# Softmax attention units: the order of two ScalarE steps, and the number of identity products at the entry

## The chip, the core and the metric

The kernel runs on one core of a Trainium2 chip. What is measured is the device time of one execution, in microseconds (us); lower is better. The time before is 1359.41 us, the median of 3 runs (1358.11 to 1360.12). The engines are called PE (TensorE, matrix products and transposes), ACT or ScalarE, DVE or VectorE, POOL (GpSimd) and SP (which issues DMAs). Each works through its own queue in order, and they wait for one another by semaphores.

## What is computed

One decoder layer for 1024 tokens of width 1024, in float32. The part that matters here is the softmax attention of four heads (the "MLA" group), with queries and keys of 192 (128 and 64 rotary) and values of 128:

```python
def causal_softmax_attention(q, k, v):
    S = q.shape[1]
    scale = MLA_QK_DIM ** -0.5
    outs = []
    for i in range(S // BLOCK_Q):          # blocks of 128 queries
        q0 = i * BLOCK_Q
        kend = q0 + BLOCK_Q
        s = jnp.einsum('bthd,bshd->bhts', q[:, q0:kend], k[:, :kend]).astype(jnp.float32) * scale
        causal = jnp.arange(kend)[None, :] <= (q0 + jnp.arange(BLOCK_Q))[:, None]
        p = jax.nn.softmax(jnp.where(causal, s, -jnp.inf), axis=-1)
        outs.append(jnp.einsum('bhts,bshd->bthd', p.astype(v.dtype), v[:, :kend]))
    return jnp.concatenate(outs, axis=1)
```

Ahead of it stand the input projection, the up-projection of queries and keys and their rotation; behind it a second kind of attention ("stick-breaking", eight heads), the output projection and a feed-forward part.

## The kernel before

The tokens lie in reverse order, so query block `qt` has 8 - `qt` key blocks of 128. Matrix products of full precision are made from three: each operand is split into a high part (a copy in the narrower format, made by ScalarE) and a low part (the difference, made by VectorE), and `three` sums high*high, high*low and low*high (lines L1691 to L1693).

**The softmax stage** is a loop over 32 units, written out by hand. A unit is one head and one query block: two phases `p` of 16 units `v` each, in the order of blocks 1, 7, 3, 5, 6, 4, 8, 2 for each head (`BLOCKS`). Unit `u` goes this way:

1. PE makes the scores (`mla_scores`) into a PSUM pair, banks 0 and 1 or 2 and 3 in turn. Scores `u` wait for exponential `u - 2`, which read that pair.
2. VectorE takes the negative row maximum `nmx` (L1393).
3. ScalarE takes the exponential into `pm` (L886), two buffers in turn, with the row sums in a second instruction. It waits for the maximum, and for the turn `u - 2`, which read that buffer.
4. PE turns (transposes) the blocks of `pm` into banks 4 and 5 (`mla_turn`, L1934). It waits for exponential `u` and for both copies of unit `u - 1`.
5. ScalarE copies bank 4 into `pmT` (`mla_copy`, L827), VectorE copies bank 5 (L1377; a unit of one block has none). `G0` is the number of blocks in ScalarE's half.
6. PE multiplies with the values (`mla_values`, L1945), and VectorE divides by the row sum (`mla_finish`).

PE's order is, for each `n`: scores `n + 2`, turn `n`, values `n - 1`. VectorE's is: maximum `u`, copy `u - 2`, finish `u - 3`, and a low split where there is one. ScalarE's is: exponential `u`, copy `u - 2`, and a high split where there is one (`SPLIT_AT`, and a few by name): the operands of the next head are split in between, 1024 columns at a time.

**The entry** to the stage: after the last of the eight up-projection tiles PE works off `WARM_MLA` products of a bf16 identity with itself into bank 0 (L1898), whose result nobody reads. Then it makes the scores of units 0 and 1, for which the first high and low splits must be there, turns the last tile of queries and keys (L1858 to L1862), and goes on with the scores of unit 2 once ScalarE and VectorE have brought that tile out (`turn_out`, L761, L774).

**Behind the stage** PE goes on to the stick-breaking units without a stop: their scores follow those of the last softmax units in the same loop, and ScalarE makes the last two softmax copies in its first two stick-breaking steps.

Of the kernel before, what the change touches and what calls it, by code (L numbers as in the profile page):

```python
# [106 lines left out]
NU = len(UNITS)  # L107
# [1 line left out]
QKL = {6: (0, 1), 7: (1, 1), 8: (0, 2), 9: (1, 2), 10: (2, 1), 11: (3, 1), 12: (2, 2), 13: (4, 1)}  # L109
NM, NS = MH // 2 * NU, SBH // 2 * NU  # L110
WARM = 40
WARM_MLA = 44
BLOCKS = [NT - i for _, i in UNITS]
G0 = [(b + 1) // 2 for b in BLOCKS]
G1_BEFORE = [sum(b > 1 for b in BLOCKS[:k]) for k in range(NU + 1)]
# [18 lines left out]
def build(nc, xT, cols_d, rows_d, pos_d, ada1_d, ada2_d, win_d, qup_d, kvup_d, wout_d, gu_d, down_d, x2_d, t_d, qkl_d, out_d):  # L134
# [155 lines left out]
    def pair(b, n=S):  # L290

        return ps[:, b:b + 2, :].rearrange("p b n -> p (b n)")[:, 0:n]
# [23 lines left out]
    def after(n):  # L316

        return n + 1 + PRIME
# [7 lines left out]
    def maxima(done, recips):  # L326

        return min(done, NM) + recips + PRIME
# [309 lines left out]
    def _(act):  # L638
# [103 lines left out]
        def mla_split(what, p, e, t=slice(0, S)):  # L742

            if p:
                act.wait_ge(sem["m_qk"], after(NU * (p - 1) + (7 if e == 0 else NU - 1)))
            dst, src = {"r": (mrH[p], QRK[:, p, t]), "q": (mqH[e], QN[:, 2 * p + e, t]), "k": (mkH[e], KN[:, 2 * p + e, t])}[what]
            A(dst[:, t], src, ACT.Copy).then_inc(sem["m_h"], 1)

        def rope_key_high(e):

            o = slice(64 * e, 64 * e + 64)
            A(KRH[e][o, :], QRK[o, 2, :], ACT.Copy).then_inc(sem["kr_h"], 1)

        def turn_out(tt):

            act.wait_ge(sem["tr_done"], after(tt))
            if tt == NT - 2:
                turn_rope(tt)
                act.wait_ge(sem["t_act"], 2 * tt + 1 + PRIME)
                mla_split("r", 0, 0, EARLY)  # L760
            A(QN[:, :, token_tile(tt)], ps[:, 4, :].rearrange("p (h n) -> p h n", h=MH), ACT.Copy).then_inc(sem["t_act"], 1)  # L761
            if tt < NT - 2:
                turn_rope(tt)
            elif tt == NT - 2:
                act.wait_ge(sem["t_act"], 2 * tt + 2 + PRIME)
                mla_split("q", 0, 0, EARLY)
                act.wait_ge(sem["t_dve"], after(tt))
                mla_split("k", 0, 0, EARLY)
            else:
                turn_rope(tt)  # L770
# [46 lines left out]
        def first_split(t):  # L817

            for what in "rqk":
                mla_split(what, 0, 0, t)  # L820

        def mla_copy(u, v):

            act.wait_ge(sem["m_tr"], after(u))
            act.wait_ge(sem["m_av"], after(u - 2))
            n = G0[v] * P
            A(pmT[v % 2][:, 0:n], ps[:, 4, 0:n], ACT.Copy).then_inc(sem["m_ta"], 1)  # L827
# [52 lines left out]
        def mla_step(u):  # L880

            p, v = divmod(u, NU)
            n = BLOCKS[v] * P
            act.wait_ge(sem["m_max"], maxima(u + 1, max(0, u - 3)))
            act.wait_ge(sem["m_tr"], after(u - 2))
            A(pm[v % 2][:, 0:n], pair(2 * (v % 2), n), ACT.Exp, bias=nmx[:, v:v + 1],  # L886
              accum_out=den[:, v:v + 1]).then_inc(sem["m_exp"], 1)
            if u >= 2:
                mla_copy(u - 2, (u - 2) % NU)
            if u == 0:  # L890
                turn_out(NT - 1)
            if u == 2:
                act.wait_ge(sem["t_act"], 2 * NT + PRIME)
                act.wait_ge(sem["t_dve"], after(NT - 1))
                first_split(LATE)
            if u == 4:
                rope_key_high(1)
            if (p, v) in SPLIT_AT:
                mla_split(*SPLIT_AT[p, v])
# [39 lines left out]
        for u in range(NM):  # L939
            mla_step(u)  # L940
# [743 lines left out]
    def _(pe):  # L1684
# [211 lines left out]
        pe.wait_ge(sem["q_copied"], NT)  # L1896
        for _ in range(WARM_MLA):
            mm(ps[:, 0, 0:P], identb[:], identb[:], start=True, stop=True)  # L1898
# [393 lines left out]
```

## Time and profile before

| what | value |
|---|---|
| median of 3 runs | 1359.41 us (1358.11 to 1360.12) |
| profiled execution, own time | 1355.37 us |
| its span (first to last instruction) | 1353.6 us |
| mean granted clock of PE | 0.998 of full |
| PE busy | 1299.7 us, 96% of the span |
| VectorE busy | 805.9 us, 60% |
| ScalarE busy | 557.8 us, 41% |
| softmax stage | about 311 to 430 us of the span |

All rows come from one profiled execution. A row of the timeline gives the start, the length, the engine, the line, the operation with its output and input, how many were merged, and in brackets how long the engine stood idle ahead of it and what released it. Instructions on one engine overlap a little, so one can start before the end of the one before. A granted clock of 1.00 is PE's full 2.4 GHz, 0.50 is 1.2 GHz. Times in the text are us from the start of the span.

### The profile page before, as it was taken

The page shows a single profiled execution, that of the slowest core. Times are in us where ns is not written, and L with a number is a line of the kernel's source. Part 1 is how long each engine was busy: PE and PEld are TensorE (multiplying, and loading weights), DVE is VectorE, ACT ScalarE, POOL GpSimd, SP SyncE. Part 2 cuts the span into 40 slices and gives each one's busy share as a digit, 9 for nine tenths or more (in the row PEclk, how much of TensorE's full clock was granted, in tenths as well). Part 3 has the DMA queues.
Part 4 walks back from the last instruction along what each step waited for, and adds up shares of the span by engine and source line. Part 5 has one row for each costly group of instructions (what it writes and reads, how often), then busy time and mean ns, then how long its engine had stood idle before and what let it go on. Part 6 is the DMA issues. An engine that isn't in the chain of part 4 may idle for free.

```text
span 1353.6 us, 17167 instructions
## 1 busy us (share of the span) xinstructions
PE 1299.7 (96%) x6708; PEld 1082.0 (80%) x6708; DVE 805.9 (60%) x1096; ACT 557.8 (41%) x912; POOL 63.7 (5%) x71
## 2 busy tenths in 40 slices
PE   3999999998999999999999999999999999999998
PEld 2688878896888888888767888888888888887886
DVE  7534667686557888953579666556665643334333
ACT  4512212685435788951364333333333322322221
POOL 1100200131000001000000000000000000001001
PEclk9999999999999999999999999999999999999999
DMA  9253445100011333501142221222212145447443
GB/s 380 102 207 136 181 173 183 47 1 1 2 40 40 78 79 79 188 16 47 45 173 93 94 94 54 87 94 94 70 71 94 62 163 178 149 140 264 140 147 125
DMA packets 38989, 149.25 MB, mean 110 GB/s; under 512 B 4352, under 2 KB 4480, under 8 KB 37376
## 3 DMA queue, kind: packets, MB, share of 16 engines
q1 hardware_dynamic: 36576, 139.80, 30.3%
q0 software_dynamic: 2336, 8.39, 1.7%
q8 instruction: 52, 0.85, 0.3%
q14 instruction: 25, 0.20, 0.1%
HBM read 117.77 MB, written 24.12 MB: 105 GB/s over the span
## 4 chain that ended last, share of the span: by engine, by line
PE 87%; DVE 6%; ACT 3%; issue 2%; DMA 1%; POOL 1%; SPq 0%; DVEq 0%; ACTq 0%; POOLq 0%
PE ps L2190 28%; PE ps L1702 13%; PE ps L1691 11%; PE ps L1693 10%; PE ps L1692 10%; PE ps L1967 3%; PE ps L1945 2%; PE ps L1954 2%; PE ps L1912 1%; DVE left L1414 1%; PE ps L1934 1%; PE ps L1913 1%; DVE beta L1419 1%; ACT omb L920 1%; DMA ada<-ada 1%
## 5 line engine op out<-in xcount | busy, mean ns | idle before, releaser
L1691 PE MATMUL ps<-TH,dWH 128*128 128x512 f32 x352 | 137.1, 390 | 0.9 <-DVE yst L1666 0.9
L1693 PE MATMUL ps<-TH,dWL 128*128 128x512 f32 x352 | 137.0, 389 | 0.0
L1692 PE MATMUL ps<-TL,dWH 128*128 128x512 f32 x352 | 137.0, 389 | 0.0
L2190 PE MATMUL ps<-h2H,slH 128*128 128x512 f32 x320 | 124.6, 389 | 0.0
L2190 PE MATMUL ps<-h2H,slL 128*128 128x512 f32 x320 | 124.5, 389 | 0.0
L2190 PE MATMUL ps<-h2L,slH 128*128 128x512 f32 x320 | 124.5, 389 | 0.0
L1625 DVE TENSOR_TENSOR TL<-traw,TH 128x512 fp32r<-128x512 f32 x44 | 30.5, 693 | 134.6 <-ACT TH L1048 134.6
L1028 ACT ACTIVATE slH<-ssum 128x512 fp32r<-128x512 f32 x80 | 50.4, 632 | 140.4 <-PE ps L2190 96.4
L1048 ACT ACTIVATE TH<-traw 128x512 fp32r<-128x512 f32 x44 | 27.8, 632 | 164.1 <-PE ps L1693 155.7
L1414 DVE TENSOR_TENSOR_SCAN left<-omb 128x255 f32<-128x255 f32 (+4 forms) x64 | 86.5, 1352 | 9.9 <-ACT omb L920 9.0
L1691 PEld LDWEIGHTS ps<-TH,dWH 128*128 128x128 f32 x352 | 66.1, 188 | 15.5 <-DVE yst L1666 1.3
L1693 PEld LDWEIGHTS ps<-TH,dWL 128*128 128x128 f32 x352 | 66.1, 188 | 13.8
L1692 PEld LDWEIGHTS ps<-TL,dWH 128*128 128x128 f32 x352 | 66.1, 188 | 13.4
L1967 PE MATMUL ps<-VS,wT 128*128 128x64 f32 x576 | 71.3, 269 | 0.1
L2190 PEld LDWEIGHTS ps<-h2H,slH 128*128 128x128 f32 x320 | 60.1, 188 | 12.7 <-issue 0.3
L2190 PEld LDWEIGHTS ps<-h2L,slH 128*128 128x128 f32 x320 | 60.1, 188 | 12.5
L2190 PEld LDWEIGHTS ps<-h2H,slL 128*128 128x128 f32 x320 | 60.1, 188 | 12.4
L1967 PEld LDWEIGHTS ps<-VS,wT 128*128 128x128 f32 x576 | 69.2, 192 | 0.2 <-issue 0.2
L1603 DVE TENSOR_TENSOR slL<-ssum,slH 128x512 fp32r<-128x512 f32 x80 | 54.9, 688 | 18.2 <-ACT slH L1028 18.2
L1125 DVE TENSOR_TENSOR WL<-raw,WH 128x1024 fp32r<-128x1024 f32 x34 | 43.2, 1269 | 32.4 <-ACT WH L648 32.3
L1603 DVE TENSOR_TENSOR slL<-sraw,slH 128x512 fp32r<-128x512 f32 x60 | 41.2, 689 | 35.4 <-ACT slH L1028 35.4
L1627 DVE TENSOR_TENSOR dWL<-draw,dWH 128x1024 fp32r<-128x1024 f32 x44 | 53.9, 1226 | 11.0 <-ACT dWH L1050 11.0
(325 smaller groups left out, 3030.4 us busy)
## 6 DMA issues: line engine op xcount, KB each, us to landing
ada<-ada SPq DMA_DIRECT2D x12, 2048.0 KB, 9.3
draw<-down SPq DMA_DIRECT2D x44, 512.0 KB, 3.7
sraw<-gu SPq DMA_DIRECT2D x20, 1024.0 KB, 5.9
raw<-win SPq DMA_DIRECT2D x22, 512.0 KB, 4.8
traw<-t_spill_d SPq DMA_DIRECT2D x44, 256.0 KB, 3.9
t_spill_d<-tst SPq DMA_DIRECT2D x20, 512.0 KB, 3.0
x_in<-xT SPq DMA_DIRECT2D x4, 1024.0 KB, 8.3
qkl_spill_d<-qkl SPq DMA_DIRECT2D x8, 512.0 KB, 3.4
```

What stands on the lines that cost most here:

```text
L1028: A(slH[q][:], operand(u, q), ACT.Copy).then_inc(sem["g_h"], 1)
L1125: V.tensor_tensor(WL[par % 2][:], raw[r % 2][:], WH[par % 2][:], ALU.subtract).then_inc(sem["split_l"], 1)
L1414: V.tensor_tensor_scan(left[v % 2][:, 1:n], omb[v % 2][:, 0:n - 1], omb[v % 2][:, 0:n - 1], 1.0, ALU.mult, ALU.bypass).then_inc(sem["s_sca ...
L1603: V.tensor_tensor(slL[q][:], operand(u, q), slH[q][:], ALU.subtract).then_inc(sem["g_l"], 1)
L1625: V.tensor_tensor(TL[d % 2][:], traw[d % 2][:], TH[d % 2][:], ALU.subtract).then_inc(sem["tl_done"], 1)
L1627: V.tensor_tensor(dWL[d % 2][:], draw[d % 2][:], dWH[d % 2][:], ALU.subtract).then_inc(sem["d_l"], 1)
L1691: mm(out, lh, rh, start=first, stop=False)
L1692: mm(out, lh, rl, start=False, stop=False)
L1693: return mm(out, ll, rh, start=False, stop=last)
L1702: last = mm(ps[:, b + hf, :], l[s][:, j * P:(j + 1) * P], cut(r, j, half(hf)), start=(j == 0 and k == 0), stop=(j == KD - 1 and k == 2))
L1967: last = mm(ps[:, bank, c:c + SBD], wT[v % 2][:, k * P:(k + 1) * P], VS[:, qt + k, (2 * i + e) * SBD:(2 * i + e + 1) * SBD], start=(k == 0 ...
L2190: last = mm(ps[:, Q_BANK[q], :], l[q][:, w], r[:, c, :], start=(c == 0 and k == 0 and q not in (Q_G2, Q_S4)), stop=(c == 3 and k == 2), sk ...
```

## The change

`WARM_MLA` becomes 84 instead of 44. In ScalarE's step of a softmax unit the copy of unit `u - 2` is put ahead of the exponential of unit `u` and of the waits of that exponential. The last two softmax copies, which are made in the first two stick-breaking steps, stay where they are.

```diff
@@ -109,7 +109,7 @@
 WARM = 40
-WARM_MLA = 44
+WARM_MLA = 84
@@ -881,12 +881,12 @@
 
             p, v = divmod(u, NU)
             n = BLOCKS[v] * P
+            if u >= 2:
+                mla_copy(u - 2, (u - 2) % NU)
             act.wait_ge(sem["m_max"], maxima(u + 1, max(0, u - 3)))
             act.wait_ge(sem["m_tr"], after(u - 2))
             A(pm[v % 2][:, 0:n], pair(2 * (v % 2), n), ACT.Exp, bias=nmx[:, v:v + 1],
               accum_out=den[:, v:v + 1]).then_inc(sem["m_exp"], 1)
-            if u >= 2:
-                mla_copy(u - 2, (u - 2) % NU)
             if u == 0:
                 turn_out(NT - 1)
```

## Rows read from the trace of the kernel before

**Rows 1.** The page: busy time of PE; shares by engine of the chain that ended last.
```profile
PE 1299.7 (96%) x6708; PEld 1082.0 (80%) x6708; DVE 805.9 (60%) x1096; ACT 557.8 (41%) x912; POOL 63.7 (5%) x71
...
PE 87%; DVE 6%; ACT 3%; issue 2%; DMA 1%; POOL 1%; SPq 0%; DVEq 0%; ACTq 0%; POOLq 0%
```

**Rows 2.** Stretches: length, busy time by engine, PE's clock, DMA share, GB/s.
```profile
312.80:316.20 3.40, 3.40 (x12) 2.69 (x11) 1.08 (x5) 0.46 (x2) 0.00 (x0) 0.50 0.00 0
...
320.00:430.00 110.00, 104.08 (x744) 91.22 (x743) 62.68 (x136) 48.29 (x112) 2.03 (x4) 1.00 0.11 25
```

**Rows 3.** Who waited for whom, 305 to 430 us: total us, times, longest.
```profile
ACT pm L886 <- DVE nmx L1393: 48.3, 21, 3.6
...
ACT pm L886 <- PE ps L1934: 12.3, 10, 2.1
...
PE ps L1934 <- ACT pmT L827: 3.2, 2, 2.2
...
PE ps L1934 <- ACT pm L886: 1.8, 5, 0.4
```

**Rows 4.** Timeline of PE at the entry.
```profile
305.54 2.62 PE L1898 MATMUL ps<-identb 128*128 128x128 bf16 x44
311.17 0.30 PE L1691 MATMUL ps<-mkH,mqH 128*128 128x128 f32 x1 [3.02 <-issue]
...
318.34 0.44 PE L1691 MATMUL ps<-mkH,mqH 128*128 128x384 f32 x1 [0.96 <-ACT QRK L774]
```

**Rows 5.** Timeline of VectorE and ScalarE at the entry.
```profile
309.99 1.08 DVE L1316 TENSOR_TENSOR mkL<-KN,mkH 128x896 fp32r<-128x896 f32 x1
...
317.42 0.60 ACT L761 ACTIVATE QN<-ps 128x512 f32<-128x512 f32 x1 [3.01 <-PE ps L1862]
```

**Rows 6.** Timeline of PE in the softmax stage: turns L1934, one scores start.
```profile
321.82 0.95 PE L1934 MATMUL ps<-ident,pm 128*128 128x128 f32 x7
...
326.86 0.47 PE L1691 MATMUL ps<-mkH,mqH 128*128 128x512 f32 x1
...
328.73 0.74 PE L1934 MATMUL ps<-ident,pm 128*128 128x128 f32 x5 [0.16 <-issue]
...
337.94 0.63 PE L1934 MATMUL ps<-ident,pm 128*128 128x128 f32 x4 [2.21 <-ACT pmT L827]
...
355.35 0.52 PE L1934 MATMUL ps<-ident,pm 128*128 128x128 f32 x3 [0.95 <-ACT pmT L827]
...
366.00 0.63 PE L1934 MATMUL ps<-ident,pm 128*128 128x128 f32 x4 [0.42 <-ACT pm L886]
```

**Rows 7.** Timeline of ScalarE in the softmax stage.
```profile
322.89 0.79 ACT L886 ACTIVATE pm<-ps,nmx 128x640 f32<-128x640 f32 x1 [1.10 <-DVE nmx L1393]
...
323.67 0.59 ACT L827 ACTIVATE pmT<-ps 128x512 f32<-128x512 f32 x1
324.15 1.06 ACT L747 ACTIVATE mqH<-QN 128x1024 fp32r<-128x1024 f32 x1
...
328.25 0.37 ACT L827 ACTIVATE pmT<-ps 128x256 f32<-128x256 f32 x1
328.65 1.05 ACT L752 ACTIVATE KRH<-QRK 64x1024 fp32r<-64x1024 f32 x1
...
337.36 0.48 ACT L827 ACTIVATE pmT<-ps 128x384 f32<-128x384 f32 x1
...
354.66 0.59 ACT L827 ACTIVATE pmT<-ps 128x512 f32<-128x512 f32 x1
```

**Rows 8.** Line L827: lengths in ns (least, median, most), first and last start.
```profile
L827 ACT ACTIVATE pmT<-ps x32: 267/426/592, 320.9 to 425.6; 128x128 f32<-128x128 f32 x8, 128x512 f32<-128x512 f32 x8, 128x256 f32<-128x256 f32 x8, 128x384 f32<-128x384 f32 x8
```

**Rows 9.** Timeline of VectorE in the softmax stage.
```profile
335.00 1.22 DVE L1393 TENSOR_REDUCE nmx<-ps 128x1 f32<-128x1024 f32 x1
336.13 0.55 DVE L1377 COPY pmT<-ps 128x384 f32<-128x384 f32 x1
...
353.76 0.55 DVE L1377 COPY pmT<-ps 128x384 f32<-128x384 f32 x1
```

## The prediction

> **What bounds the kernel now.** I read the page first: PE is busy 1299.7 of 1353.6 us and 87% of the chain that ended last lies on it [rows 1]. So a change is worth what it takes out of PE's idle time or gives back of PE's clock, and the question is where PE stands still near the two edits. The view by stretches puts both there: from 312.8 to 316.2 us PE is fully busy, at a granted clock of 0.50 (the 1.2 GHz level), and over the softmax stage, 320 to 430 us, at 1.00, with 104.08 busy of 110 us, so 5.9 us are idle [rows 2]. The view of who waited for whom names the idle time: PE's turn of the probabilities (L1934) waits 3.2 us in two places for the copy L827 and 1.8 us in five that are put down to the exponential L886. ScalarE itself waits 48.3 us for VectorE's maxima and 12.3 us, in ten places, for PE's turns [rows 3]. ScalarE has room, but in what order it works decides when PE goes on.
>
> All these stalls are of one kind. The turn of unit n needs the exponential n and both halves of the copy n-1 (ScalarE's L827, VectorE's L1377), since it overwrites the PSUM banks 4 and 5. In ScalarE's queue the copy n-1 stands behind the exponential n+1, which needs the maximum n+1. In the timeline the copy of 0.48 us that begins at 337.36 ends at 337.84 and PE starts at 337.94, after 2.21 idle; the copy of 0.59 from 354.66 ends at 355.25 and PE starts at 355.35, after 0.95 [rows 6, 7]. The five put down to the exponential start in the same way 0.10 us after the copy's end (one stands in [rows 6], 366.00, with 0.42 idle; they sum to the 1.8). The eighth, 0.16 us at 328.73, starts 0.11 after the end of the copy at 328.25 [rows 6, 7].
>
> **Edit 1, 40 more identity products.** 44 of them take 2.62 us from 305.54, so 0.06 us each; then PE stands still for 3.02 us until 311.17 [rows 4], because the split that the first scores need (DVE mkL) ends at 311.07 [rows 5]. 40 more at 2.46/44 = 0.056 each last 2.24 us and end near 310.4, 0.77 us ahead of that: they cost nothing, and that 0.77 is their cover (if the splits came 1 us earlier, they would cost 0.2). The idle stretch shrinks from 3.02 to 0.77. In this trace the clock falls once: 1.6 us after that 3.02 idle. After 2.21 idle (337.94) and 0.96 idle (318.34) it stays at 1.00 [rows 2, 4, 6], so I take it that it doesn't fall. What this gives: 3.40 us at half clock is 1.70 us of excess; I take 1.6, as the ends of the stretch are known only to about one matmul. It counts in full, since what comes next waits for this work: ScalarE's turn_out (317.42) waits 3.01 us for PE's transposes, the third unit's scores (318.34) wait for that [rows 4, 5]. From there everything is earlier together. Bounds: 0 (the clock falls anyway) to 1.7.
>
> The Trainium skill, "TensorE: Matmul & The Clock Gate", in the part on transposes, says that the transpose mode doesn't count as busy for the clock. By that rule the transposes and the pause ahead of 318.34 could bring on a fall of their own, now that the one before is gone. The trace speaks against it: the clock rose at 316.2 and stayed up across just those transposes and the pause of 0.96 us. By the rule the entry's gain would be near zero.
>
> **Edit 2, the copy ahead of the exponential.** Nothing is added: the same 32 copies and 32 exponentials run, no DMA and no other queue is passed, the splits stay behind both. The copy u-2 waits for the turn u-2, for which the exponential u waited too (its buffer), and for the values u-4, which PE has issued before that turn; so no new wait ends late. What changes:
>
> (a) The copy runs in the idle time ahead of the maximum, and no longer ends any of the eight waits. What is late next is VectorE's half of the copy, which stays behind the maximum, or PE's own work.
>
> (b) Where a split follows, it starts one copy earlier, and so do the low split and the next maximum, which close a ring (exponential, copy, split, low split, maximum, exponential).
>
> (c) Where the turn u-2 ends last, the exponential comes later by the copy: 0.27 to 0.59 us [rows 8].
>
> The long stall, step by step, in the times of before. The turn of unit 1 ends at 322.77 [rows 6]. Copy 1 now starts there instead of at 323.67, and the exponential of 322.89 moves 0.48 behind it (0.59 less the overlap of 0.11 seen between 323.67 and 324.15) to 323.30, 0.41 late. Three splits then lose the copy ahead of them: 0.48 (323.67 to 324.15), 0.40 (328.25 to 328.65), 0.37 (a copy of 384 columns, 0.48 as at 337.36, less 0.11) [rows 7]. The maximum of 335.00 comes at 335.00 + 0.41 - 1.25 = 334.16, VectorE's copy behind it at 336.13 - 0.84 = 335.29 and ends at 335.84 [rows 9]; with 0.10 PE could turn at 335.94. PE's own scores end at 335.73 (337.94 less 2.21), or 335.57 with the 0.16 of the first stall gone. So PE turns at 335.94 instead of 337.94: 2.0 us for the two stalls, with 0.4 left of the long one, ended by VectorE's copy.
>
> The 0.95 at 355.35: two splits lie ahead in its ring (0.16 + 0.16 for two copies of 0.27); VectorE's copy ends at 353.76 + 0.55 - 0.32 = 353.99 [rows 9]. PE's own end is 355.35 - 0.95 = 354.40, less 0.25 from the stall before it: 354.15. Both are there together: 0.95 gone, with nothing to spare. The five short ones, 1.8 in all: the turn that such a copy wants has ended well ahead of it, and VectorE is named in one wait of PE only, at the end of the stage; all gone. Sum: 2.0 + 0.95 + 1.8 = 4.7 us.
>
> Point (c) costs nothing by my reading: the exponential u is wanted by the scores u+2, and the closest case is the first: the exponential of 323.30 ends by 324.2 (0.79 long, and its sum), and its scores start at 326.86, 2.7 us later [rows 6]. Bounds: a gain of 5.1 (all stalls) to a loss, priced below. The handover to the next stage (one stall of 0.17 us by VectorE) and all behind it is chained to PE, and is carried along.
>
> In sum 1.6 + 4.7 = 6.3 us. Profiled, that is 1355.4 - 6.3 = 1349.1 us (span 1347.3). That execution lies 4.0 below the median of the runs shown; against the median the forecast is 1359.4 - 6.3 = **1353.1 us**, a change of -0.46%. A measurement of this kernel can tell about 0.2% (2.7 us) from no change.
>
> **The rivals.**
> - *The clock falls anyway*, by the page's rule or otherwise; only edit 2 works: 1359.4 - 4.7 = 1354.7. For it: one fall in the trace is thin evidence, and the timed runs may stand differently. Against: 0.77 us idle is less than pauses without a fall. 12%.
> - *The waits move to VectorE.* The ring doesn't shorten, only ScalarE's copy does: the long stall ends at 336.68 + 0.10 with VectorE's copy (gain 1.2 of 2.2), the next at 354.41 (0.9), the short ones go (1.8), the first stays: 3.9, with the clock 5.5: 1353.9. If half of the short ones stay also: 3.0, with the clock 4.6: 1354.8. For it: VectorE's copy and splits stand behind maxima, next in line everywhere. 14%.
> - *The gain is given back in the next stage*, where ScalarE and VectorE are busy for most of the time: what is early there waits for them. Then only some 1.5 us are left: 1357.9, no change by the bound. Against: those engines' work there starts from PE's scores too, nothing is tied to an absolute time. 8%.
> - *Slower: the exponential takes the copy's place.* The ten exponentials that wait for PE's turn come a copy later, ten times 0.43 (the median copy [rows 8]) = 4.3 us, if the scores or the turn n have no slack for it; then the stalls at the turn aren't recovered either. 1359.4 + 4.3 - 1.6 = 1362.1; without the clock 1363.7; all 32 copies on the path would make 13.6 and 1371. It decides once the slack of 2.7 us at the closest place is less than a copy. Against: it is over four times the longest copy. 6%.
>
> **How the numbers follow.** My forecast: 60%, its own range 1352.0 to 1354.4 (clock 1.2 to 1.7, stalls 4.0 to 5.1, 0.5 of scatter). The range reaches over the first two rivals and the scatter of the runs: 1351.0 to 1356.6, leaving out the last two and a little of the rest. Faster by over 0.2% (below 1356.7) holds in the forecast and two rivals, 0.85 less a little for mixed cases; within 0.2% 0.1; slower 0.06.
>
> **What would show it.** Right: 84 products end near 310.4 with under 1 us idle behind; the clock is 1.00 from 308 to 320; the third unit's scores start near 316.7; PE's waits for L827 in the softmax stage are gone, and what is left there (0.4 us) is put down to VectorE's L1377; the copy begins before the exponential; ScalarE's idle time stands ahead of both. The stage's idle time is some 1.2 us instead of 5.9. Wrong: a clock below 1 after 312 us; waits of PE on L886 with a true length; more idle time after 430 us.

## The result, and the profile after

The changed kernel takes 1349.11 us, the median of 4 executions (1348.95 to 1351.58); the kernel before took 1359.74 beside it (4 executions, 1358.11 to 1360.12). The ratio is 0.9934, with a 95% interval of 0.9915 to 0.9953. It isn't the quotient of the two medians, which is 0.9922: by the medians the gain is 10.6 us, by the ratio 9.0 (6.4 to 11.6). The forecast was 1353.1 with a range of 1351.0 to 1356.6: the direction was right, the gain was above the 6.3 forecast either way, and the time lies outside the range. The profiled execution, though, has a span of 1347.4 us, and the prediction had said 1347.3 for it. So profile against profile the forecast holds, and median against median it doesn't. That gap is what the experiments are about.

The page's row of busy time: PE's 1298.9 us are nearly those of [rows 1], in a shorter span.

```profile
PE 1298.9 (96%) x6748; PEld 1082.6 (80%) x6748; DVE 805.8 (60%) x1096; ACT 559.9 (42%) x912; POOL 63.7 (5%) x71
```

Stretches of the changed kernel, against [rows 2] (length; busy time of PE, PEld, DVE, ACT, POOL; PE's clock; DMA share; GB/s):

```profile
312.80:316.20 3.40, 3.40 (x23) 2.88 (x21) 2.46 (x7) 0.46 (x2) 0.00 (x0) 1.00 0.00 0
320.00:430.00 110.00, 107.37 (x783) 94.91 (x782) 68.49 (x143) 54.61 (x117) 2.03 (x4) 1.00 0.11 25
```

The clock stays at 1.00 over the entry, and PE is busy 107.37 us of the second stretch instead of 104.08 (it now reaches some 8 us into the next stage). Who waited for whom, 305 to 430 us, and in the last row over the whole span for PE (total us, times, longest):

```profile
ACT pmT L827 <- PE ps L1934: 37.4, 25, 3.1
...
ACT pm L888 <- DVE nmx L1393: 14.9, 16, 1.7
...
PE ps L1934 <- DVE pmT L1377: 1.0, 2, 0.8
```

PE no longer waits for ScalarE's copy or exponential (L886 is now L888); both rows on PE in [rows 3] are gone. ScalarE's idle time now stands ahead of the copy, which waits for its turn, where it costs nothing. The view names two waits of PE in the stage, both for VectorE's half of the copy. Over the stretch from 320 to 430 us PE is idle for 2.63 us; 1.47 of these stand in three pauses of the next stage (0.62 at 421.38, 0.49 at 425.30 and 0.36 at 428.05), which leaves 1.16 where 1.2 was forecast. PE's timeline, against [rows 4] and [rows 6]:

```profile
306.07 4.85 PE L1898 MATMUL ps<-identb 128*128 128x128 bf16 x84
311.70 0.30 PE L1691 MATMUL ps<-mkH,mqH 128*128 128x128 f32 x1 [0.78 <-issue]
...
317.33 0.44 PE L1691 MATMUL ps<-mkH,mqH 128*128 128x384 f32 x1 [0.96 <-ACT QRK L774]
...
335.10 0.63 PE L1934 MATMUL ps<-ident,pm 128*128 128x128 f32 x4 [0.85 <-DVE pmT L1377]
...
347.76 0.95 PE L1934 MATMUL ps<-ident,pm 128*128 128x128 f32 x7
...
351.28 0.52 PE L1934 MATMUL ps<-ident,pm 128*128 128x128 f32 x3
...
361.35 0.60 PE L1934 MATMUL ps<-ident,pm 128*128 128x128 f32 x4
...
421.38 0.30 PE L1954 MATMUL ps<-ident,beta 128*128 128x128 f32 x1 [0.62 <-issue]
```

This gives the gain of each part by the start times of the same instruction in both traces. The first scores come 0.53 us later than in the kernel before (311.70 against 311.17); the identity products already start that much later (306.07 against 305.54), so it comes from the stages ahead, where nothing was changed. From them to the third unit's scores it is 5.63 us instead of 7.17: 1.54 from the clock. From there to the first stick-breaking turn, which stood at 428.00 before, it is 104.05 instead of 109.66: **5.61 from the new order**. Behind that 0.4 is lost again, in a wait of PE for a weight split. A wait of this kind, 0.4 to 0.6 us long, stands in six of the thirteen traces, two of the old order (e1, g3) and four of the new, and is missing in the other seven: it is scatter. 0.53 - 1.54 - 5.61 + 0.4 = -6.2, the difference of the spans. That this meets the forecast of 6.3 is partly luck: the new order brought 0.9 more than its share of the sum, and 0.9 of scatter took it away again.

```profile
428.00 0.30 PE L1954 MATMUL ps<-ident,beta 128*128 128x128 f32 x1 [0.51 <-issue]
```

### The profile page after: what moved, and what is told of

It is laid out like the page before. It is cut to its first block, busy times and chain, and to the rows that moved or that the text cites. A ratio compares the mean times of both kernels' runs of the same rounds, so it can differ in the third digit from the quotient of the medians.

```text
span 1347.4 us, 17247 instructions
## 1 busy us (share of the span) xinstructions
PE 1298.9 (96%) x6748; PEld 1082.6 (80%) x6748; DVE 805.8 (60%) x1096; ACT 559.9 (42%) x912; POOL 63.7 (5%) x71
## 4 chain that ended last, share of the span: by engine, by line
PE 85%; DVE 7%; ACT 3%; issue 2%; DMA 2%; POOL 1%; SPq 0%; DVEq 0%; ACTq 0%; POOLq 0%
PE ps L2190 28%; PE ps L1702 13%; PE ps L1691 10%; PE ps L1693 10%; PE ps L1692 10%; PE ps L1967 3%; PE ps L1954 2%; PE ps L1945 2%; PE ps L1912 1%; DVE left L1414 1%; PE ps L1913 1%; PE ps L1934 1%; DMA traw<-t_spill_d 1%; DVE beta L1419 1%; ACT omb L920 1%
```

## The experiments

The kernel before ran 59 times beside the experiments, on three chips. Its times, grouped by the mean clock of the execution, already say where the missing 4 us are:

| mean clock of PE | executions of before | time, us |
|---|---|---|
| 0.998 | 15 | 1355.2 to 1356.0 |
| 0.996 | 16 | 1356.9 to 1358.7 |
| 0.995 | 12 | 1357.8 to 1358.8 |
| 0.994 | 16 | 1359.3 to 1360.8 |

The profiled execution of the kernel before was one of the first row. An estimate from the table: 0.998 less 0.994, of 1357 us, is 5.4 us of clock, and the executions of the last row are 4.6 us longer (medians 1360.1 and 1355.5). The mean clock is a rough guide, though, as it also counts a fall that costs nothing: in every trace the clock goes to 0.50 once more behind PE's last product, 2.0 to 5.3 us after its end, when PE has nothing left to do. In the trace of the changed kernel that product ends at 1341.15:

```profile
1344.00:1346.00 2.00, 0.00 (x0) 0.00 (x0) 0.00 (x0) 0.00 (x0) 0.00 (x0) 0.50 0.38 145
```

In the kernel before it starts at 1350.45, so its trace has two falls and not one, and its 0.998 is both of them together. The theories:

- **A**: in the timed executions the clock falls in more places than the profile showed; which of them, varies. The change takes places away.
- **B**: the gap of 4 us between profile and median is a matter of chip or execution and has nothing to do with the change.

### One part alone

**e1**, only the first edit, in the kernel before:

```diff
-WARM_MLA = 44
+WARM_MLA = 84
```

> Only the 84 identity products; the copy stays behind the exponential. Theory A (the timed executions of before lose time to clock falls that its profiled one doesn't show, and the shorter idle time at the entry takes some of them away): clearly more than 1.6 us, some 4 to 6 us below before, and a mean clock of the timed executions of before that is lower than the 0.998 of its profile. Theory B (the 4 us between profile and timed executions of before are a matter of the chip or of the execution and have nothing to do with the change): 1.5 us below before. In the profile of both theories: third unit's scores 1.5 us sooner after the first scores, the eight stalls in the softmax stage as before.

Measured: 1357.64 us, 12 executions of 1356.10 to 1359.13, clock 0.996 to 0.998; before 1358.55 (1355.25 to 1360.80). Ratio 0.9994 (0.9984 to 1.0005). Neither the 4 to 6 us of A nor the 1.5 of B: 0.9 us by the medians, nothing that can be told from no change. Its trace shows that the entry isn't the only place. PE's timeline and two stretches of e1:

```profile
336.81 0.63 PE L1934 MATMUL ps<-ident,pm 128*128 128x128 f32 x4 [2.21 <-ACT pmT L827]
...
312.80:316.20 3.40, 3.40 (x22) 2.75 (x21) 2.47 (x6) 0.46 (x2) 0.00 (x0) 1.00 0.00 0
...
336.20:340.60 4.40, 3.79 (x21) 3.83 (x22) 1.08 (x4) 1.34 (x6) 0.00 (x0) 0.63 0.00 0
```

The fall at the entry is gone (1.00), and there is one behind the long stall of 2.21 us: a mean of 0.63 over 4.4 us is 3.3 us at half clock. So A needs a wider form: there are more places than the entry, and closing this one gives far less than 4 us. Whether the fall at the long stall stood there instead of the one at the entry, or would have been there in any case, one trace can't show; e4 below has both. The prediction had taken just this pause, because the clock held after it in the one trace, as a sign that such a pause is harmless.

**e2**, only the second edit, with 44 products (the diff of the change without its first hunk).

> Only the copy ahead of the exponential, with 44 identity products. By the change's own profile this part brings 5.6 us (the shift of PE between the third unit's scores and the first long stick-breaking turn). Theory A: 5.6 us, or more if a clock fall in the timed executions of before belongs to the 2.2 us stall at 338. Theory B: 5.6 us, and e1 and e2 add up to what before loses in its profile, not to the 10.6 us measured. The clock falls once after the entry, as in before.

Measured: 1352.67 us, 6 executions of 1348.52 to 1355.14, clock 0.993 to 0.999. Ratio 0.9948 (0.9931 to 0.9964), which is 7.1 us of 1358.55; by the medians it is 5.9. Both fit A (5.6 or more), and 5.9 fits B's 5.6 as well. B's sum doesn't decide either: e1 and e2 add up to 6.8 us by the medians and 7.9 by the ratios, against the 6.2 between the two profiled executions and the 10.6 measured. The fastest of the six took 1348.52 with a clock of 0.999. The profiled execution was the slowest. PE's timeline and two stretches:

```profile
32.48 0.77 PE L1770 MATMUL ps<-hH,WH 128*128 128x512 f32 x1 [2.16 <-ACT hH L666]
...
315.22 0.44 PE L1691 MATMUL ps<-mkH,mqH 128*128 128x128 f32 x1 [3.02 <-issue]
...
32.00:38.70 6.70, 5.62 (x20) 1.76 (x20) 3.02 (x4) 3.73 (x4) 0.00 (x0) 0.51 0.97 405
...
315.40:321.00 5.60, 5.60 (x19) 4.69 (x20) 2.49 (x9) 1.36 (x3) 0.00 (x0) 0.50 0.01 3
...
320.00:322.00 2.00, 2.00 (x9) 1.90 (x8) 0.27 (x1) 0.00 (x0) 0.00 (x0) 0.53 0.00 0
```

Two things are new. There is a third place, near 30 us, which neither kernel's first profile showed: a pause of 2 us in the input stage, and 6.8 us at half clock that begin inside it, at 31.8. And a fall at the entry can be 6.8 us long (315.1 to 321.9), not 3.4, though the pause ahead is the same 3.02 us: from the first scores to the third unit's it is 8.69 us in this trace, 7.17 in the kernel before and 5.63 without a fall.

**e4**, the kernel before with no products at the entry (`WARM_MLA = 0`).

> The kernel before with no identity products at the entry at all: PE stands still for 5.5 us instead of 3.0. Leaves no part of the computation out. The clock falls at least as long: Theory A: also in the timed executions a longer or earlier fall, 1 to 4 us slower than before. Theory B: 0 to 2 us slower, one fall.

Measured: 1359.86 us, 12 executions of 1356.69 to 1360.42, ratio 1.0005 (0.9994 to 1.0016). By the medians it is 1.3 us slower, which fits both theories. Its trace has falls in all three places (from 32.0, 311.9 and 342.6 us, the last behind the long stall, which ends at 341.48 here). The 44 products of the kernel before, which leave 3 us idle behind them, were worth nothing that can be told from no change.

### The places filled one by one

PE's idle time can be filled with identity products that nobody reads, without a change to what the other engines do. So each place can be closed alone.

**f1**, the changed kernel once more, on another chip.

> The changed kernel once more, beside the kernel before on one chip. By the profiles so far the clock can fall in three places: at 30 to 38 us (near the kernel's start, in the traces of e2, e3 and e4), at the stage's entry near 312 and behind the long stall near 338. Theory A: the changed kernel can only fall in the first: some executions at 1349.0 with a mean clock of 0.999, others 2 to 4 us above with 0.996 to 0.998, median 1349 to 1351; ratio to before 0.993 to 0.995. Theory B (execution scatter is something else than the clock): time and mean clock of the executions don't go together.

Measured: 1350.99 us (1350.13 to 1351.95, 5 executions, clock 0.997 to 0.999) beside 1358.07 of before (15 executions, 1355.30 to 1360.28). Ratio 0.9945 (0.9932 to 0.9959): 7.1 us by the medians, within 1 us of the forecast's 6.3. Median and ratio are where A had them, and time and clock go together, but none of the five was as fast as 1349.0. Its trace has one fall, near 30 us (this stretch):

```profile
32.00:38.00 6.00, 5.18 (x28) 1.95 (x27) 3.37 (x4) 2.36 (x3) 0.00 (x0) 0.72 0.98 407
```

So the 1349.11 of the first comparison was partly luck. Three of its four executions took 1348.95 to 1349.15 with a clock of 0.999; the one of them that was profiled has no fall in the input stage, and by their times the other two had none either. And none of the four of before was of the fastest kind (1358.11 was the lowest).

**f2**, the kernel before with 84 products, and the long stall filled:

```diff
+            if n == 5:
+                for _ in range(38):
+                    mm(ps[:, 3, 0:P], identb[:], identb[:], start=True, stop=True)
             turned(n)
```

> The kernel before with 84 products, and 38 more identity products into the free bank 3 ahead of the turn of unit 5, where PE stands still 2.2 us (2.1 us of products, hidden in that wait). The order on ScalarE is the old one and all eight stalls keep their length. Theory A: the clock no longer falls near 338; executions without a fall near the start take 1353.8 (1355.4 less 1.6), the others 1356 to 1358, median 1.5 us or more below e1 (1357.6). Rival: the clock doesn't fall there because of the pause, or the products delay the turn: 1357 to 1358 as e1.

Measured: 1355.98 us, 11 executions of 1354.20 to 1357.23. Ratio 0.9985 (0.9976 to 0.9994), against e1's 0.9994. As A expected, 1.7 us below e1's median, though on another chip (1.2 us by the ratios, whose intervals overlap), and the lowest time is at 1354. Its trace has a fall near 30 us and none at 338.

**f3**, the changed kernel with the pause near 29 us filled:

```diff
+        for _ in range(30):
+            mm(ps[:, 0, 0:P], identb[:], identb[:], start=True, stop=True)
         pe.wait_ge(sem["split_l"], 2)
         for n in range(KD + LAG):
```

> The changed kernel with 30 identity products (1.7 us) in PE's pause of 1.9 us near 29 us, the only place left where its clock fell before the end. Theory A: all executions at 1349.0 to 1349.5 with a clock of 0.999, median up to 1.5 us below the changed kernel's on this chip. Rival: the fall there stems from the stretch of products with one column ahead of the pause, or the 30 products end late: as the changed kernel or up to 0.5 us slower.

Measured: 1348.77 us, 5 executions of 1348.26 to 1349.15, all with a clock of 0.999. Ratio 0.9928 (0.9914 to 0.9941). 2.2 us below f1 on the same chip, and the two don't overlap (f1's lowest is 1350.13). That is more than the 1.5 expected, and the rival, that the products of one column ahead bring on the fall whatever stands in the pause, is refuted: f3's trace has no fall near 30.

**g1**, the old order with all three places filled (the additions of f2 and f3 together).

> The kernel before (old order on ScalarE) with all three pauses filled by identity products: 30 near 29 us, 84 at the stage's entry, 38 ahead of the turn of unit 5. Theory A: no fall in any execution, all within 1 us of 1354.2, mean clock 1.000 or 0.999; the difference to f3 (1348.8), 5.4 us, is then the pure worth of the new order, and the 5.5 us of scatter of the kernel before are gone. If a good part of the scatter stays, it isn't the clock's.

Measured: 1354.33 us, 11 executions of 1353.84 to 1355.05, ratio 0.9980 (0.9971 to 0.9989). The kernel before ran from 1355.24 to 1359.97 on the same chip: a spread of 4.7 us has become 1.2. This is the plainest evidence for A: nothing but PE's idle time was filled. In g1's trace the clock is 1.00 from PE's first product to its last, which ends at 1346.30. It falls only behind that, at 1348.28, and this alone makes the mean 0.998, below the 1.000 or 0.999 expected; the two slowest executions, 1354.67 and 1355.05, have 1.000. The products stand in the old stall and delay nothing: the turn behind them comes 19.61 us after the third unit's scores, against 19.60 in the kernel before. The products:

```profile
334.62 2.29 PE L2077 MATMUL ps<-identb 128*128 128x128 bf16 x38
```

It also gives the two parts apart. Without falls the old order takes 1354.33 and the new one 1348.77 (f3): 5.6 us, as the two first traces have it (5.61). The two ran on different chips; by their ratios, 0.9980 and 0.9928, it would be 0.5% or 7 us, with intervals of 1.2 and 1.8 us to either side.

**g2**, the new order, 44 products at the entry, the pause near 29 us filled.

> The new order with 44 products at the entry, and 30 near 29 us: only the entry is left as a place of falls. Theory A: a fall there in every execution, of 3.4 us (1.6 lost) or twice as long as in the trace of e2 (3.3 lost): 1350.4 to 1352.2, so 1.6 to 3.4 us above f3; this is what 84 instead of 44 are worth in the new order.

Measured: 1350.43 us, 5 executions of 1350.18 to 1351.91, clock 0.997 to 0.999, ratio 0.9956 (0.9940 to 0.9972); 1.7 us above f3, which ran on another chip. By its median the range was just met (1350.4 to 1352.2, and the lowest is below it), but not the "every execution": PE's timeline and a stretch of its profiled execution show the pause of 3.02 us with no fall behind it.

```profile
312.45 0.30 PE L1691 MATMUL ps<-mkH,mqH 128*128 128x128 f32 x1 [3.02 <-issue]
...
312.00:320.00 8.00, 6.59 (x41) 5.64 (x42) 5.46 (x13) 4.11 (x9) 1.83 (x2) 1.00 0.00 1
```

That execution took 1350.18 us all the same, 1.3 us more in span than f3's profiled one (1348.4 against 1347.1). 0.3 of it is there by the first scores and 0.6 is a wait of PE for a weight split in the last stage, which f3's trace doesn't have. So there is scatter of about 1 us that isn't put down to the clock, and the 1.7 us of g2 can't all be put down to the entry's falls.

**g3**, the kernel before with only the pause near 29 us filled.

> The kernel before with 30 products near 29 us: entry and the long stall are left as places of falls. Theory A: 1355.3 to 1358.5, median 1.5 to 2 us below before; the highest times of before, 1359.8 to 1360.8 with a clock of 0.994, are gone, since they need a fall near the start as well.

Measured: 1356.34 us, 11 executions of 1355.73 to 1359.39, ratio 0.9993 (0.9983 to 1.0003), beside 1357.48 of before. Ten of the eleven lie below 1357, but one at 1359.39 stands above what was expected, and the gain of 1.1 us is less than the 1.5 to 2 expected; the ratio can't be told from 1. That one has the same clock, 0.997, as executions of 1355.73 and 1355.83: its 3 us aren't the mean clock's, and what they are isn't shown. Its trace has no fall at the entry and one behind the long stall. Filling one place of three moves the median by about 1 us, as in e1. The three add up: 0.9 us for the entry (e1), 1.1 for the input stage (g3), 1.2 for the long stall (f2's 2.1 less e1's 0.9), in sum 3.2, all by the medians on their own chips; all three at once gave 3.15 (g1, 1357.48 to 1354.33). Each by itself is at the edge of what can be told from no change.

### The wait that is left

**e3** and **f4**: the changed kernel, and f3, with VectorE's copy of unit 4 ahead of the maximum of unit 6:

```diff
+            if u == 6:
+                mla_copy((u - 2) // NU, (u - 2) % NU)
             dve.wait_ge(sem["m_qk"], after(u))
             V.reduce_max(nmx[:, v:v + 1], pair(2 * (v % 2), n), axis=AX.X, negate=True).then_inc(sem["m_max"], 1)
-            if u >= 2:
+            if u >= 2 and u != 6:
                 mla_copy((u - 2) // NU, (u - 2) % NU)
```

> The changed kernel, and VectorE's copy of unit 4 ahead of the maximum of unit 6, the one place where PE still waits (0.85 us) for VectorE's copy. If that copy is all that stands in the way, PE turns at its own end: 0.8 to 1.0 us below the changed kernel, some 1348.2. Rival: the maximum of unit 6, 0.5 us later, makes the exponential and what hangs on it late, and nothing or less is left of it.

> f3 and the edit of e3 (VectorE's copy of unit 4 ahead of the maximum of unit 6). If the 0.85 us of PE's wait are worth their length: 0.8 us below f3, near 1348.3, and the best of all. Rival: the later maximum gives it back: as f3.

Measured: e3 1350.62 us (1348.00 to 1352.76, 6 executions), ratio 0.9940 (0.9924 to 0.9957), with a fall near 30 us in its trace; beside f1's 1350.99 on another chip nothing is decided. f4 1348.46 us (1347.93 to 1348.99, 5 executions), f3 1348.77 on the same chip; both have the ratio 0.9928. In f4's trace the turn of unit 5 no longer waits, and two rows on a new wait stands there:

```profile
333.98 0.61 PE L1938 MATMUL ps<-ident,pm 128*128 128x128 f32 x4
...
336.13 0.33 PE L1693 MATMUL ps<-mkH,mqH 128*128 128x128 f32 x1 [0.21 <-ACT pm L888]
```

From the third unit's scores to the turn of unit 6 it is 19.71 us in f4 (317.22 to 336.93) and 20.26 in f3: 0.55 of the 0.85 remain as a gain, and the scores of unit 8 now wait for the exponential of unit 6, which the later maximum delays. That is the rival's mechanism, at part of its price. f4 had the lowest median of all kernels, 9.6 us below the kernel before on its chip, but its 0.3 us over f3, where 0.8 was expected, are within the scatter.

## Why the prediction was right or wrong

**Which waits the new order removes: right.** All eight stalls were put down to the copy behind the exponential, and all are gone. ScalarE's timeline of the changed kernel has the order, against [rows 7], VectorE's the ring:

```profile
321.80 0.60 ACT L827 ACTIVATE pmT<-ps 128x512 f32<-128x512 f32 x1 [1.18 <-PE ps L1934]
322.30 0.79 ACT L888 ACTIVATE pm<-ps,nmx 128x640 f32<-128x640 f32 x1
...
323.07 1.06 ACT L747 ACTIVATE mqH<-QN 128x1024 fp32r<-128x1024 f32 x1
...
332.39 0.49 ACT L827 ACTIVATE pmT<-ps 128x384 f32<-128x384 f32 x1 [0.29 <-PE ps L1934]
334.52 1.11 ACT L888 ACTIVATE pm<-ps,nmx 128x1024 f32<-128x1024 f32 x1 [1.64 <-DVE nmx L1393]
```
```profile
333.27 1.22 DVE L1393 TENSOR_REDUCE nmx<-ps 128x1 f32<-128x1024 f32 x1
334.40 0.55 DVE L1377 COPY pmT<-ps 128x384 f32<-128x384 f32 x1
```

The exponential of unit 3 starts 0.50 behind its copy, where 0.48 was reckoned. The time frame has moved by 1.01 us (318.34 to 317.33). The ring's steps gave 334.16 for the maximum and 335.94 for the turn; less 1.01 these are 333.15 and 334.93, and the trace has 333.27 and 335.10. That VectorE's copy is next in line was right too (0.85 us left instead of 0.4: PE's own work ended 0.3 sooner, and the turn came 0.17 later). The rival in which the ring doesn't shorten is refuted by the same rows, and so is the slower rival: PE waits nowhere for the exponential in the changed kernel.

**The sum of the stalls: 4.7 forecast, 5.6 measured.** The first two gave 1.83 (2.0 forecast), the one of 0.95 gave 0.82, as PE's turn of that unit is at 351.28 instead of 355.35 and the one before it at 347.76 instead of 351.01. The five short ones are the term that was mis-sized. They were priced at their idle time, 1.8 in all. By start times they gave 0.42, 0.59, 0.41, 0.59 and 0.58, 2.6 in all, each 0.16 more than its idle time. The reason is in the rows: a product of 128 columns lasts 0.27 us in the view, but the next starts 0.11 later when none waits, so the last of a group still counts as busy for 0.16 us of a wait. Besides, the view prints no idle time below some 0.15 us (0.16 is the least in these rows), so a wait of some 0.3 us by start times can be missing from it. One such was in the kernel before, ahead of the turn of unit 19: 0.14 us are idle there, without a bracket, and its distance from the turn ahead fell from 3.66 to 3.34 (before, then after):

```profile
382.31 0.49 PE L1934 MATMUL ps<-ident,pm 128*128 128x128 f32 x3
...
385.97 0.74 PE L1934 MATMUL ps<-ident,pm 128*128 128x128 f32 x5
```
```profile
377.22 0.49 PE L1934 MATMUL ps<-ident,pm 128*128 128x128 f32 x3
...
380.56 0.71 PE L1934 MATMUL ps<-ident,pm 128*128 128x128 f32 x5
```

1.83 + 0.82 + 2.59 + 0.32 = 5.56; the rest, to 5.61, is rounding and small shifts. The stall of 0.95 doesn't fit the rule of 0.16: its removal should have given 1.11. The missing 0.29 is such a hidden wait that is left in the changed kernel. From the turn at 347.76 to that at 351.28 it is 3.52 us, where the same pair takes 3.24 in the last head (399.90 to 403.14), and PE starts 0.14 behind the end of VectorE's copy (350.59 + 0.55), as it does at 335.10, 0.15 behind the end of the copy that starts at 334.40. The prediction had PE and that copy ready together, "with nothing to spare"; the copy is late by this much.

**The clock at the entry: right in the trace, wrong as a rule.** The prediction reads that the clock falls once; it falls twice, but the second time behind PE's last product, where it costs nothing. 1.6 us were forecast for the first, 1.54 in the trace. The 84 products end 0.78 us ahead of the scores (0.77 forecast). That the clock doesn't fall behind transposes and the pause of 0.96 us held as well: it is 1.00 there in the changed kernel, with no fall ahead of it. So the rule of the Trainium skill that transposes don't count ("TensorE: Matmul & The Clock Gate", the part on transposes) had no effect here that could be seen, over ten transposes and one pause. But the step "falls after 3.02 us idle, holds after 2.21" failed both ways. In the traces of e1 and g3 the clock fell after the 2.21, in those of g2 and g3 it held after the 3.02.

**From the profile to the median: the step that failed.** The prediction carried the 4.0 us between the profiled execution and the median of before over to the changed kernel as a constant. They were falls of the clock in places that this one execution had been spared. The slower executions of before were not traced themselves; that it was falls rests on the table, on the traces of e1, e2 and e4, and on g1, where filled pauses took them away. The change closes two of the three places: none of the five traces with both edits (the changed kernel, e3, f1, f3, f4) has a fall at the entry or near 335. With g1 and f3 as the times without falls, the typical loss is 1357.8 - 1354.3 = 3.5 us before (median of 59 executions) and 1350.3 - 1348.8 = 1.5 us after (median of the 9 executions of this kernel). So the change is worth 5.6 us by its order and 2.0 by the clock, in sum about the 7.5 between the two medians, as far as times from different chips can be set beside each other; the forecast of 6.3 was 1.2 short, 0.9 of it in the stalls and the rest in the clock. The other 3.1 of the 10.6 measured at first are the draw of four executions each.

**The gain given back in the next stage:** refuted. From the first stick-breaking turn to the end it is 926.0 us after and 925.6 before, and the 0.4 is the wait for the weight split.

## What to carry to other kernels

When the profiled execution isn't near the median, ask for the difference before forecasting across it: compare the mean clock of all executions, not one trace. Price a stall by start-to-start distances, not by the idle time in the view. And products that keep PE's clock up were worth about 1 us for each pause in the old order, too little to be told from no change one at a time, and 3 us together. What was tried with success fills a pause nearly to its end; 44 products with 3 us idle behind them gave nothing that could be told. With the new order and no pause left open the kernel is 9.3 us below before, with a spread of 0.9 us instead of 5 (f3).

## What the runs showed of the hardware

- The same pause is followed by a fall of the granted clock in some executions and not in others. After the 3.02 us at the entry there was none (g2, g3), one of 3.4 us (before) or one of 6.8 us (e2). After the 2.21 us at the long stall it held at 1.00 (before) or went to 0.50 for 3.3 us by the stretch shown (e1).
- Falls explain most of the scatter of this kernel: 5.6 us over 59 executions, 1.2 us with PE's three pauses filled (g1), 0.9 us in the new order (f3). What is left, about 1 us, lies partly in PE's waits for weight splits (0 to 0.6 us in the last stage). One execution of g3 was 3 us slower than others of the same mean clock, for a reason that isn't shown.
- With a pause of 2 us in the input stage, behind products of one column, five of eight traces have a fall of the clock there (e1, the kernel before and the changed kernel have none), up to 6.8 us long (e2). With 30 identity products in the pause none of five traces has one (f3, f4, g1, g2, g3).
- Behind PE's last product the clock falls in every trace, 2.0 us (g1) to 5.3 us (f4) after its end. This costs nothing, but it is in the mean clock.
